# A depthwise convolution of width 31: one of its four channel tiles is given to GpSimd, the other three stay on VectorE

## What is computed

```python
def causal_dwconv(x_ext, w, b):
    ch = x_ext.shape[-1]
    y = lax.conv_general_dilated(x_ext, w[:, None, :], window_strides=(1,), padding='VALID',
                                 dimension_numbers=('NWC', 'WIO', 'NWC'), feature_group_count=ch)
    return y + b

glu = a_in * jax.nn.sigmoid(a_gate)
conv_ext = jnp.concatenate([conv_hist, glu], axis=1)
y_a = jax.nn.silu(layer_norm(causal_dwconv(conv_ext, conv_w, conv_b), conv_ln_g, conv_ln_b))
...
merged = (gates[:, :, 0] * (y_a @ w_branch[0]) + gates[:, :, 1] * (y_b @ w_branch[1])
          + gates[:, :, 2] * (y_c @ w_branch[2]))
```

## Time and profile before

| | us |
|---|---|
| median of 3 runs (lowest, highest) | 1905.36 (1904.74, 1905.58) |
| the profiled execution, its own time | 1909.57 |
| its span, first to last instruction | 1907.8 |
| TensorE's mean granted clock in it | 0.983 |
| TensorE busy (matmuls) | 1837.0 (96%) |
| VectorE busy | 1137.9 (60%) |
| ScalarE busy | 770.1 (40%) |
| GpSimd busy | 5.4 (0%) |
| the 240 tap instructions of VectorE (L1026) | 176.9 us recorded, 806 ns each |

### The profile page before, as it was taken

How to read it: one execution, slowest core, us unless ns; L and a number is a source line. 1 busy time by engine, 2 the same in 40 slices (tenths; PEclk the granted TensorE clock), 3 DMA queues, 4 the chain that set the end, 5 groups by cost and what they waited for, 6 DMA issues and landing times.

```text
span 1907.8 us, 32749 instructions
## 1 busy us (share of the span) xinstructions
PE 1837.0 (96%) x14392; PEld 1786.0 (94%) x14392; DVE 1137.9 (60%) x1744; ACT 770.1 (40%) x1215; POOL 5.4 (0%) x20
## 2 busy tenths in 40 slices
PE   7999999989999999999999999999899999999997
PEld 7978999989999999999998889899899999999996
DVE  3256689765675444446642657997657754444466
ACT  3355332244355444434533543222534644444342
POOL 0000000000000000000000000000000000000000
PEclk9999999989999999999999999999899999999998
DMA  6311112212213222255533111222222222222543
GB/s 228 109 73 45 59 63 90 71 67 78 89 67 111 89 89 89 83 165 179 171 139 113 45 45 59 81 76 78 67 89 89 79 99 89 89 89 84 182 161 130
DMA packets 36366, 186.00 MB, mean 97 GB/s; under 512 B 7360, under 2 KB 11712, under 8 KB 17920
## 3 DMA queue, kind: packets, MB, share of 16 engines
q1 hardware_dynamic: 34560, 178.34, 27.4%
q10 hardware_dynamic: 1664, 5.57, 0.7%
HBM read 176.75 MB, written 7.15 MB: 96 GB/s over the span
## 4 chain that ended last, share of the span: by engine, by line
PE 77%; DVE 13%; ACT 5%; DMA 3%; issue 2%; ACTq 0%; DVEq 0%
PE acc L1456 23%; PE acc L1461 23%; PE acc L1462 23%; DVE acc L1026 6%; DVE wl L861 2%; DMA v_out<-vfm 1%; PE small L1577 1%; PE turned L1556 1%; PE score L1527 1%; ACT wh L445 1%; ACT xT L479 1%; ACT xh L480 1%; DMA xT<-x_in 1%; DMA raw<-win 1%; PE score L1529 1%
## 5 line engine op out<-in xcount | busy, mean ns | idle before, releaser
L1456 PE MATMUL acc<-xh,wh 128*128 128x272 f32 x2944 | 866.1, 294 | 22.9 <-DVE xl L828 8.3
L1461 PE MATMUL acc<-xl,wh 128*128 128x272 f32 x2944 | 854.9, 290 | 0.0
L1462 PE MATMUL acc<-xh,wl 128*128 128x272 f32 x2944 | 854.3, 290 | 0.0
L1456 PEld LDWEIGHTS acc<-xh,wh 128*128 128x128 f32 x2944 | 562.9, 191 | 28.4 <-DVE wl L861 10.2
L1461 PEld LDWEIGHTS acc<-xl,wh 128*128 128x128 f32 x2944 | 562.2, 191 | 0.3
L1462 PEld LDWEIGHTS acc<-xh,wl 128*128 128x128 f32 x2944 | 560.6, 190 | 0.0
L861 DVE TENSOR_TENSOR wl<-raw,wh 128x2048 fp32r<-128x2048 f32 (+2 forms) x157 | 325.2, 2071 | 244.9 <-ACT wh L445 244.8
L445 ACT ACTIVATE wh<-raw 128x2048 fp32r<-128x2048 f32 (+2 forms) x175 | 306.8, 1753 | 166.8 <-DMA raw<-wdn 114.5
L1456 PE MATMUL acc<-fhh,wh 128*128 128x272 f32 x704 | 204.7, 291 | 3.0 <-DVE xT L1274 1.8
L1462 PE MATMUL acc<-fhh,wl 128*128 128x272 f32 x704 | 202.6, 288 | 0.0
L1461 PE MATMUL acc<-fll,wh 128*128 128x272 f32 x704 | 202.4, 287 | 0.0
(11 more groups left out here) (215 smaller groups left out, 2193.2 us busy)
## 6 DMA issues: line engine op xcount, KB each, us to landing
raw<-win SPq DMA_DIRECT2D x51, 1024.0 KB, 5.0
raw<-wup SPq DMA_DIRECT2D x44, 1024.0 KB, 4.9
raw<-wdn SPq DMA_DIRECT2D x32, 1024.0 KB, 4.9
raw<-wbr SPq DMA_DIRECT2D x24, 512.0 KB, 3.6
raw<-wdn SPq DMA_DIRECT2D x16, 768.0 KB, 4.2
raw<-wout SPq DMA_DIRECT2D x8, 1024.0 KB, 5.0
k_out<-k ACTq DMA_DIRECT2D x2, 1088.0 KB, 9.4
v_out<-vfm ACTq DMA_DIRECT2D x2, 1088.0 KB, 11.6
```

The source lines that it names most:

```text
L1456: first = mm(out, a, xs[0], start=start, stop=False)
L1461: mm(out, a, xs[1], start=False, stop=False)
L1462: return mm(out, b, xs[0], start=False, stop=stop)
```

## The change

The last channel tile (m = 3) of taps 1 to 30 leaves VectorE. GpSimd computes it: for each tap one product (`tensor_scalar`, glu times the weight, into one of two buffers `prod`) and one addition (`tensor_tensor`, acc plus the product, in place). Each addition waits for its product (`conv_prod`) and for the addition before (`conv_tile`); each product, from the third on, waits until the addition before last has read its buffer. GpSimd starts when tap 0 is written (`glu_full`, 4). VectorE's `tap` loops over three tiles, and VectorE waits for GpSimd's 30 additions of the layer once, ahead of the copy L1237. The two buffers, 574 columns each, lie in the memory of `sqc`, which is written only in the normalisation behind that wait.

```diff
+        prod = [sb(f"prod{i}", [P, CV], at=F + 90016 + i * 2304) for i in range(2)]
...
+        conv_tile = sem("conv_tile")
+        conv_prod = sem("conv_prod")
...
                 g.affine_select(out=wsgu[:, :, :], in_=wsgu[:, :, :], compare_op=ALU.is_ge, fill=0.0, base=0,
                                          pattern=[[0, CT], [1, P]], channel_multiplier=-1).then_inc(
                                              sgu_masked, c.up(sgu_masked))
+
+                m = CT - 1
+                pool.wait_ge(glu_full, c.take(glu_full, CT))
+                for j in range(1, WID):
+                    part = prod[j % 2][:, 0:CV]
+                    if j > 2:
+                        pool.wait_ge(conv_tile, c.seen(conv_tile, 1))
+                    g.tensor_scalar(part, glu[:, m, j:j + CV], col(par, PAR["conv_w"] + j * CT + m), None,
+                                    ALU.mult).then_inc(conv_prod, c.up(conv_prod))
+                    pool.wait_ge(conv_prod, c.seen(conv_prod))
+                    if j > 1:
+                        pool.wait_ge(conv_tile, c.seen(conv_tile))
+                    g.tensor_tensor(acc[:, m, :], acc[:, m, :], part, ALU.add).then_inc(conv_tile, c.up(conv_tile))
...
             def tap(j):
 
-                for m in range(CT):
-                    dve.wait_ge(vec, c.seen(vec, CT - 1))
+                for m in range(CT - 1):
+                    dve.wait_ge(vec, c.seen(vec, CT - 2))
                     v.scalar_tensor_tensor(out=acc[:, m, :], in0=glu_at(m, j), scalar=col(par, PAR["conv_w"] + j * CT + m),
                                                in1=acc[:, m, :], op0=ALU.mult, op1=ALU.add).then_inc(vec, c.up(vec))
...
                 dve.wait_ge(vec, c.seen(vec))
+                dve.wait_ge(conv_tile, c.take(conv_tile, WID - 1))
                 v.tensor_copy(st2[:, 0:P].rearrange("p (a n) -> p a n", a=CT), acc[:, :, SCOL:SCOL + DEC]).then_inc(
                     vec, c.up(vec))
```

## The result

| | before | with the change |
|---|---|---|
| median, us (lowest, highest) | 1905.47 (1904.74, 1907.78), 4 runs | 1936.11 (1933.37, 1937.97), 4 runs |
| profiled execution, its span | 1909.57, 1907.8 | 1937.97, 1936.2 |
| mean granted clock of TensorE | 0.983 | 0.977 |
| VectorE busy | 1137.9 | 1154.2 |
| GpSimd busy | 5.4 | 230.1 |

The change makes the kernel slower: the ratio is 1.0158, 95% interval from 1.014 to 1.0175, so 30.6 us, 15.3 a layer. The forecast was 55.8 us. The sign was right and the time lies in the range, but the size is only a little over half of the forecast.

A forecast was written before the change was run, and what follows sets the result against it. TensorE works 96% of the span; VectorE bounds four tight convolution stretches and costs about 9.5 us a layer. Terms (a) to (f) sum to 27.9 us a layer, 55.8 for both, added to 1905.4: 1961 us, range 1888 to 1984.

The forecast's parts named there:

- rival 1: Both engines run at their own pace, so TensorE's waits go: 7.6 us a layer gained, 1890 us; chance 0.22.
- (a): 211 to 222.7 us: 12 tap instructions each behind one of GpSimd's, less 2.9 us removed; token copy later, +7.6 us a layer.
- (c): 236 to 254.3 us, through the token norm: 22 VectorE instructions each held 0.875 us, less 1.5 us: +17.8 us a layer.
- (b): 222.7 to 236 us: copies read PSUM, statistics one tensor, and VectorE waits for TensorE; GpSimd does some 13 more: 0.
- (d): Mixed rows to 266.6 us: up to nine VectorE instructions held, part of it beside its waits for TensorE: +4.5 us a layer.
- (e): From 266.6 us GpSimd is nearly through, TensorE bounds the tight stretches and its waits go: -4.0 us a layer.
- (f): TensorE's clock: two more long waits cost 0 to 5 us a layer, taken as +2.
- Rival 2: VectorE keeps precedence, GpSimd enters only at PSUM reads, one-tensor reads or idle time: 1891 to 1940, likeliest 1908 us; chance 0.18.
- rival 3: GpSimd is so slow, from 6 us a tap on, that the chain does not fit; at 7 us 1965 us; chance 0.05.

The follow-up runs named there:

- the memsets: The changed kernel with GpSimd's products and additions replaced by 60 memsets a layer of 128x1148, which write and read nothing: 1898.54 us, ratio 0.9966.
- the fifteen taps: The changed kernel with GpSimd given only 15 of the last tile's 30 taps, started after VectorE's last instruction on that tile: 1920.45 us, ratio 1.0076.
- the added chain in the convolution: The kernel before plus GpSimd's 30 products and 30 additions a layer on scratch memory and the wait; VectorE keeps four tiles: 1982.6 us, ratio 1.0413.

## Why the prediction was partly right

**The sign and the kind of mechanism** were right. In these runs instructions of VectorE with two inputs from SBUF and reading instructions of GpSimd get in each other's way; rival 1, both at their own pace, is refuted by the 1.29 and 1.75 us taps (0.80 undisturbed), and by the kernels with products or additions alone (taps of up to 1.30 and 1.78 us). The forecast let an instruction of the one hold up the other to its end. The trace agrees for the addition to within 0.2 us (the held tap ends 0.61 us behind it and takes 0.80 alone). It does not for the product, in the middle of which a tap of VectorE's starts and ends (213.19 to 214.48 in 212.52 to 214.87).

**The size** failed in the step "12 taps' instructions, each behind one of GpSimd's", 0.875 us each, which is used in (a) and (c). By stage, in us, a layer:

| step | forecast | measured | between |
|---|---|---|---|
| (a) taps to the token copy | +7.6 | +1.9 | 11.65 -> 13.53 |
| (b) token statistics | 0 | +1.5 | 13.30 -> 14.84 |
| (c) two taps to the end of the norm | +17.8 | +5.2 | 18.30 -> 23.54 |
| (d) mixed rows | +4.5 | +2.4 | 12.54 -> 14.95 |
| (e) tight stretches and on | -4.0 | +3.8 | 124.5 -> 128.35 |
| (f) clock | +2 | 4.2, within the rows above | |
| sum | 27.9 | 14.9 | |

(a): three additions at 0.95 and four products at 0.49 fall into it, 4.8 us of hold against 10.5 forecast, less the same saving of 2.9. (c): the 22 instructions grew by 7.7 us, 0.35 each and not 0.875; 1.0 of it went into VectorE's wait for ScalarE's `rs` (1.34 us before, 0.37 now) and 1.5 is the saving, which leaves 5.2. Two sizes were wrong behind that, in opposite directions. GpSimd was too fast in the forecast: its masks gave 0.69 us for a product of 574 columns, which takes 1.72 undisturbed; the addition, put at 1.06, takes 1.20. And the hold was too dear: not a GpSimd instruction's length per VectorE instruction, but 1.44 us per three of VectorE's, 0.48 each, because GpSimd's tap of 3.6 us holds only 1.44 of them. That the two partly cancelled is luck: with the true lengths (1.46 us for a mean instruction) the forecast's rule would have given 14.6 and 30.6 us in (a) and (c), over 90 us for both layers from these two steps alone. The range, from 1888 to 1984, was also wide enough for rival 1, a gain.

The 0.15 us of semaphore in the forecast's chain of 57 us was the smaller error. It is the gap in the trace of before between GpSimd's four selects of 32x32, each of which waits for a semaphore of the one ahead of it, 0.6 us for the four:

```profile
L416 POOL TENSOR_SCALAR_AFFINE_SELECT tmp<-tmp 32x32 f32<-32x32 f32 x4 | 0.8, 207 | 0.6
```

In the change an addition begins 0.08 us behind the end of its product (236.86 to 236.94 us), and the next product begins as the addition's record ends (214.96 + 1.32 = 216.28 us; it starts at 216.26).

**The step with the wrong sign was (e)**, "From there GpSimd is nearly through". By the end of the token norm 47 of its 60 instructions were to be done; 27 were. The remainder ran to 327.4 us, through the first two tight stretches, which grew from 21.1 and 19.35 to 25.4 and 23.2 us: waits of 4.2 and 3.3 us for L867 where 3.2 in all was to vanish. Behind these it was as forecast: twelve tap instructions in 8.80 us, and no wait over 0.3 for a low part.

**(b)** was put at nothing for its PSUM and one-input work; no row of before shows such work beside GpSimd. In the change those rows hardly grew (the copies 688 ns for 678, the statistics 694 for 694), but one weight's low part lies among them, and it took 3.07 us for 2.26; 0.4 us more is a longer wait for TensorE's fourth turn (1.81 for 1.45). GpSimd did eight instructions there, not 13. **(f)**: no run shows the forecast's 2 us of clock, or rival 1's 1 us, as a term by itself. What the change shows in its place is a TensorE that is busy 4.2 us longer a layer, at a granted clock of 0.95 for 0.98. Behind the wait of 7.2 us for the norm the granted clock is 0.68 from 262 to 282 us, with 85 matmuls in 15.93 us of busy time, 0.187 each, against 0.125 at 1.00 in the feed-forward part:

```profile
262.00:282.00 20.00, 15.93 (x85) 14.93 (x86) 15.82 (x23) 5.87 (x7) 19.58 (x11) 0.68 0.27 83
```

No experiment changed the clock alone, so how much of a wait's cost it is was read and not tested.

**The costs put at nothing** do not show in any row: the semaphores (median tap beside the memsets 814 ns, before 808), VectorE's shorter distance (811), the buffers, the wait at the end (80 us behind the last addition). Rival 2 had a part of the truth, since GpSimd does lose to VectorE (115 us for a chain that would take 30 x 2.99 = 90), and the first product of the fifteen taps waited while VectorE's instructions passed; it erred in giving VectorE precedence throughout. What rival 3 said, a chain that does not fit, came up in the fifteen taps alone.

Still open: what in a product makes its hold half an addition's, and what decides which of the two engines goes first.

## What to carry to other kernels

Before work is moved from VectorE to GpSimd beside it, set what one moved instruction saves against what it holds: here 0.73 us saved and 1.44 lost, 0.95 for a two-input addition alone, as long as VectorE works with both inputs in SBUF; single VectorE instructions with one input there were held as well (0.94 us for 0.53 beside memsets). Here the price fell on VectorE and was paid where VectorE had no slack (39 us a layer for the added chain in the convolution, 3.7 in the feed-forward part), so look for stages in which VectorE idles or reads PSUM (433 ns beside GpSimd, 436 without), and count with GpSimd at its held pace (3.6 to 4.0 us a tap, not 3.0). The wait at the end of the moved chain was free where the chain was through before it (80 us ahead in the change), and cost VectorE 10.1 us with fifteen taps, where it was not.

## What was not expected of the hardware

- GpSimd's product with one tensor in takes 1.72 us for 574 columns, its addition with two 1.20 (227.11 and 228.92 us of the change, beside VectorE's statistics), a memset of 574 columns 0.58 (in the chain beside four tiles). The longest of them holds VectorE the least of the two that read (0.49 against 0.95; up to 1.17 in the chain beside four tiles).
- Memsets of GpSimd left VectorE's two-input instructions alone (taps of 828 ns at most), and held its `tensor_scalar` from SBUF to SBUF (0.53 to 0.94 us).
- GpSimd was held in turn: a product beside a 2048-column low part took 3.77 us, beside VectorE's full queue with fifteen taps 5.87.
- In the feed-forward part copies of two columns were held as well, one to 1.18 us where before they took 0.16 to 0.17:

```profile
L1344 DVE COPY fst<-gex x44: 156/165/1175, 572.9 to 1753.8; 128x2 f32<-128x2 f32 x44
```
